# Sums over partitions by an all-ones product, square roots on ScalarE, and two running-sum products stacked into one

## The chip, the cores and the metric

One core of one Trainium2 chip runs the kernel. The metric is the device time of one execution in microseconds (us), the median of three runs.

## The reference

Two transformer blocks in a row, on 256 tokens of width 1024, in fp32. Three places matter here.

```python
# first block, state-space mixer: per head, running sums of dt*A over the tokens give the decay;
# the output is gated and normed in 8 groups of 256 channels, then multiplied by w_out
decay[i, j] = exp(cumsum[i] - cumsum[j])            # for j <= i
y = y * silu(z)
y = y * rsqrt(mean(y ** 2 over the group's 256 channels) + 1e-5) * norm_w
# second block, gated delta rule: 4 heads of 128 channels
q = l2_normalize(q) * 128 ** -0.5                   # q / sqrt(sum(q ** 2) + 1e-6)
k = l2_normalize(k)
```

Around them stand large matrix products (in-projection, two MLPs, attention, a mixture of 32 experts) whose weights come from memory once.

## The kernel before, in words

Everything is written out by hand: each engine has its own program (`block.sync`, `.scalar`, `.tensor`, `.vector`, `.gpsimd`), and they wait for one another by semaphores. Weights come in 1 MB units through a ring of six buffers. ScalarE rounds a unit to its high part (`w_hi`, line 398), VectorE subtracts to get the low part (`w_lo`, line 1656), and TensorE forms every product from three matmuls of rounded values (high by high, low by high, high by low: lines 851 to 853). Activations lie transposed, channels on partitions and tokens on the free axis, so a sum over channels is a sum over partitions.

**The scan of the state-space mixer** runs over 16 pairs of heads, hp = 0 to 15. In each step TensorE does: on every second step `scores` (lines 1004, 1005) for the next group; `running(hp + 2)` (lines 1012, 1013), which spreads each head's running sum over all partitions by a product of a picked row with the sums, once for their high and once for their low part; half a unit of the z projection (`z_half`, up to hp = 11) or a tile of the out-projection (`out_early`); `head_y(hp)` (lines 1021, 1022). VectorE forms the decay's argument (lines 1741, 1742), ScalarE its exponential (line 480), GpSimd multiplies it by the scores (line 2420), and `head_y` waits for that. ScalarE also applies silu to z (`z_read`, line 454), which needs another activation table than the exponential.

The group norm trails behind: for group g, ScalarE squares (`y_square`, line 466, odd hp), TensorE sums the squares over partitions with one column of ones as the moving operand (`group_sums`, line 1030, even hp; the result lies with tokens on partitions), VectorE scales and adds epsilon (line 1754), GpSimd raises to the power -0.5 (line 2414), TensorE turns the result and spreads it over partitions by a product with the identity (`group_scale`, line 1038, next odd hp), VectorE applies it (`y_norm`, line 1761), ScalarE and VectorE split the result (`y_high` line 471, `y_low` line 1767). `group_sums(g)` waits for `yn_done`, the end of `y_norm(g - 1)`, because both share bank 6. The last two groups are done between tiles of the out-projection.

**The delta rule** does the same for q and k: squares into `rn` (line 685; the trace shows the tile as l_rstd), 16 one-column products (line 1353), VectorE adds epsilon (line 2085), GpSimd takes the root (line 2482), and after a tile of the gate projection 16 products with the identity spread it (line 1372); VectorE applies it (line 2102). Between the two stand small running sums (line 1359) and their spread (`gb_mm`, line 1363). `gate_tile(0, 1)` stands between line 1363 and line 1372, `gate_tile(1, 0)` and `gate_tile(1, 1)` behind line 1372, and then the products of line 1385, which wait for `l2_done`.

The running sums' source `da` is written by VectorE in the softplus of unit 12 (line 1709), between two convolution units.

Of the kernel before, what the change touches and what calls it, by code (L numbers as in the profile page):

```python
# [5 lines left out]
F32 = mybir.dt.float32  # L6
# [5 lines left out]
P = 128  # L12
T = 256
# [140 lines left out]

DT_AFTER = 9
# [25 lines left out]
def build(nc, x, weights, small, consts, levels, onehot, cols, rows, ln_rows, rms_rows, b_mod, rel_bias, out):  # L181
    with ExitStack() as ctx:
# [57 lines left out]
        csT_hi = mem("sums_hi", 128, [32, T], F32R)  # L240
        csT_lo = mem("sums_lo", 129, [32, T], F32R)
        pick = mem("pick", 202, [32, 32], F32R)
# [146 lines left out]
        def _(act):  # L389
# [41 lines left out]
            A(pick[:, :], const[0:32, 0:32], ACT.Copy).then_inc(S["small_hi_done"], 1)  # L431
# [27 lines left out]
            A(csT_hi[:, :], PS[0:32, 6, 0:T], ACT.Copy).then_inc(S["csT_done"], 1)  # L459
# [21 lines left out]

            decay(0)
# [14 lines left out]
            y_square(GROUPS - 1)  # L497
            split(at("out") + 2 + AHEAD)
            y_high(6)
            y_high(7)  # L500
# [222 lines left out]
            ya_high(3)  # L723
            act.wait_ge(S["small_read"], 4 + 1)
# [121 lines left out]
        def _(pe):  # L846
# [129 lines left out]
            mm(PS[0:32, 6, 0:T], da[:, 0, :], triu_ones, start=True, stop=False)  # L976
            mm(PS[0:32, 6, P:T], da[:, 1, :], triu, start=False, stop=True).then_inc(S["small_mm"], 1)
# [29 lines left out]
            def running(hp):  # L1007

                wait(pe, S["d_read"], hp - 1)
                for c in range(2):  # L1010
                    o, one = PS[:, 2 + hp % 2, c * T:(c + 1) * T], pick[:, 2 * hp + c:2 * hp + c + 1].to_broadcast([32, P])
                    mm(o, one, csT_hi[:, :], start=True, stop=False)
                    last = mm(o, one, csT_lo[:, :], start=False, stop=True)
# [11 lines left out]
            def group_sums(g):  # L1025
                pe.wait_ge(S["sq_done"], g + 1)
                wait(pe, S["yn_done"], 2 * g)
                for t in range(TT):
                    for c in range(2):
                        last = mm(PS[:, 6, t:t + 1], ysq[:, c, t * P:(t + 1) * P], ones[:, 0:1],  # L1030
                                  start=c == 0, stop=c == 1)
                last.then_inc(S["ms_done"], 1)

            def group_scale(g):

                pe.wait_ge(S["y_rstd"], g + 1)
# [1588 lines left out]
```

## Time and profile before

| | us |
|---|---|
| median of 3 runs | 1352.01 (1351.21 to 1352.43) |
| profiled execution, its own time | 1355.23 |
| its span | 1353.4 |
| TensorE busy | 1313.4 (97%) |
| VectorE busy | 991.2 (73%) |
| ScalarE busy | 721.1 (53%) |
| GpSimd busy | 130.6 (10%) |
| mean granted TensorE clock | 0.987 of full speed |

The span is the time from the first to the last instruction of the profiled execution; the execution's own time has a little around it, and the runs without a profile are slightly shorter. A matmul in fp32 has two records in the trace, one of the rounded type one record. Records overlap, since matmuls are pipelined: the cost of one is the distance from its start to the next one's start, not its duration.

### The profile page before, as it was taken

The page shows a single profiled execution, that of the slowest core. Times are in us where ns is not written, and L with a number is a line of the kernel's source. Part 1 is how long each engine was busy: PE and PEld are TensorE (multiplying, and loading weights), DVE is VectorE, ACT ScalarE, POOL GpSimd, SP SyncE. Part 2 cuts the span into 40 slices and gives each one's busy share as a digit, 9 for nine tenths or more (in the row PEclk, how much of TensorE's full clock was granted, in tenths as well). Part 3 has the DMA queues.
Part 4 walks back from the last instruction along what each step waited for, and adds up shares of the span by engine and source line. Part 5 has one row for each costly group of instructions (what it writes and reads, how often), then busy time and mean ns, then how long its engine had stood idle before and what let it go on. Part 6 is the DMA issues. An engine that isn't in the chain of part 4 may idle for free.

```text
span 1353.4 us, 19001 instructions
## 1 busy us (share of the span) xinstructions
PE 1313.4 (97%) x8019; PEld 1151.5 (85%) x8019; DVE 991.2 (73%) x1135; ACT 721.1 (53%) x768; POOL 130.6 (10%) x118
## 2 busy tenths in 40 slices
PE   7999999999999999999999999999999999999996
PEld 7999888799998798799999798799888888888884
DVE  6978656767878735867865855747566889889896
ACT  6665764254444456544444364727324667776773
POOL 0001544200000100000000100016100000000000
PEclk9999999999999999999999998989998999999998
DMA  8543224487877543357775363421345689898992
GB/s 316 185 172 138 94 94 151 164 305 282 309 284 281 204 157 106 123 190 277 281 252 188 144 226 125 140 67 59 124 156 198 231 337 372 334 349 339 350 363 95
DMA packets 41625, 289.77 MB, mean 214 GB/s; under 512 B 4637, under 2 KB 5045, under 8 KB 7488
## 3 DMA queue, kind: packets, MB, share of 16 engines
q1 hardware_dynamic: 35712, 252.76, 50.7%
q0 software_dynamic: 5824, 35.74, 7.0%
q8 instruction: 66, 1.08, 0.3%
q14 instruction: 23, 0.19, 0.0%
HBM read 286.38 MB, written 2.11 MB: 213 GB/s over the span
## 4 chain that ended last, share of the span: by engine, by line
PE 84%; DVE 10%; ACT 3%; issue 2%; POOL 1%; DMA 0%; DVEq 0%; ACTq 0%; SPq 0%; POOLq 0%
PE banks L851 24%; PE banks L853 23%; PE banks L852 23%; DVE w_lo L1656 3%; PE banks L1419 2%; PE banks L1522 1%; ACT w_hi L398 1%; DVE conv L1702 1%; DVE qkvT L2034 1%; PE banks L1198 1%; POOL tiny L2440 1%; PE banks L1030 1%; PE banks L910 1%; DVE pre_norm L1814 1%; PE banks L1554 1%
## 5 line engine op out<-in xcount | busy, mean ns | idle before, releaser
L1656 DVE TENSOR_TENSOR w_lo<-raw,w_hi 128x2048 fp32r<-128x2048 f32 x237 | 542.2, 2295 | 110.7 <-ACT w_hi L398 109.3
L398 ACT ACTIVATE w_hi<-raw 128x2048 fp32r<-128x2048 f32 x237 | 449.9, 1909 | 17.4 <-DMA raw<-weights 17.4
L851 PE MATMUL banks<-hT_hi,w_hi 128*128 128x256 f32 x1120 | 322.6, 288 | 3.0 <-DVE w_lo L1687 3.0
L853 PE MATMUL banks<-hT_hi,w_lo 128*128 128x256 f32 x1120 | 319.7, 285 | 0.0
L852 PE MATMUL banks<-hT_lo,w_hi 128*128 128x256 f32 x1120 | 319.7, 285 | 0.0
L851 PEld LDWEIGHTS banks<-hT_hi,w_hi 128*128 128x128 f32 x1120 | 217.7, 194 | 8.3 <-issue 5.4
L852 PEld LDWEIGHTS banks<-hT_lo,w_hi 128*128 128x128 f32 x1120 | 217.8, 194 | 1.1
L853 PEld LDWEIGHTS banks<-hT_hi,w_lo 128*128 128x128 f32 x1120 | 217.7, 194 | 0.0
L851 PE MATMUL banks<-w_hi,act_hi 128*128 128x512 f32 x256 | 100.1, 391 | 0.4 <-DVE act_lo L1870 0.4
L852 PE MATMUL banks<-w_lo,act_hi 128*128 128x512 f32 x256 | 99.9, 390 | 0.0
L853 PE MATMUL banks<-w_hi,act_lo 128*128 128x512 f32 x256 | 99.6, 389 | 0.0
L851 PE MATMUL banks<-w_hi,group_T_hi 128*128 128x512 f32 x248 | 99.3, 400 | 0.0
L853 PE MATMUL banks<-w_hi,group_T_lo 128*128 128x512 f32 x248 | 97.0, 391 | 0.0
L852 PE MATMUL banks<-w_lo,group_T_hi 128*128 128x512 f32 x248 | 96.8, 390 | 0.0
L851 PE MATMUL banks<-w_hi,hT_hi 128*128 128x512 f32 (+1 forms) x240 | 90.9, 379 | 4.5 <-DVE hT_lo L1662 4.2
L853 PE MATMUL banks<-w_hi,hT_lo 128*128 128x512 f32 (+1 forms) x240 | 88.1, 367 | 0.0
L852 PE MATMUL banks<-w_lo,hT_hi 128*128 128x512 f32 (+1 forms) x240 | 88.0, 367 | 0.0
L513 ACT ACTIVATE relu<-banks 128x512 f32<-128x512 f32 x32 | 19.1, 598 | 106.2 <-PE banks L853 106.2
L1899 DVE SCALAR_TENSOR_TENSOR mod<-mod_raw,col,mod 128x512 f32<-128x512 f32 x96 | 72.1, 751 | 2.6
L2440 POOL TENSOR_TENSOR tiny<-tiny 128x1 f32<-128x1 f32 x14 | 15.5, 1107 | 587.7 <-DVE tiny L2392 315.4
L527 ACT ACTIVATE act_hi<-relu_sq 128x512 fp32r<-128x512 f32 x28 | 17.7, 633 | 87.4 <-PE banks L853 87.4
L851 PEld LDWEIGHTS banks<-w_hi,hT_hi 128*128 128x128 f32 x240 | 46.1, 192 | 14.2 <-DVE hT_lo L1662 7.0
(427 smaller groups left out, 2121.0 us busy)
## 6 DMA issues: line engine op xcount, KB each, us to landing
raw<-weights SPq DMA_DIRECT2D x238, 1024.0 KB, 4.8
mod_raw<-weights POOLq DMA_DIRECT2D x24, 1024.0 KB, 5.2
ln_gain_bias<-ln_rows POOLq DMA_DIRECT2D x4, 1024.0 KB, 8.2
h<-x SPq DMA_DIRECT2D x2, 512.0 KB, 4.3
h<-x POOLq DMA_DIRECT2D x1, 1024.0 KB, 5.5
rms_gain<-rms_rows POOLq DMA_DIRECT2D x2, 512.0 KB, 5.9
h_rows<-h POOLq DMA_DIRECT2D x1, 1024.0 KB, 4.5
bias_rows<-bias_table POOLq DMA_DIRECT2D x1, 1024.0 KB, 10.0
```

What stands on the lines that cost most here:

```text
L398: A(hi[u % RING][:, :], raw[u % RING][:, :], ACT.Copy).then_inc(S["w_hi_done"], 1)
L513: A(rbuf[e % 2][:, :], PS[:, e if e < 2 else (e + 2) % 4, :], ACT.Relu).then_inc(S["relu_done"], 1)
L527: A(aTh[e % 2][:, :, :], sbuf[e % 2][:, :].rearrange("p (c t) -> p c t", c=2), ACT.Copy).then_inc(S["act_hi"], 1)
L851: mm(out, a[0], b[0], start=start, stop=False)
L852: mm(out, a[0], b[1], start=False, stop=False)
L853: return mm(out, a[1], b[0], start=False, stop=stop)
L910: last = pe.transpose(tr_bank(0, banks + t + 2 * half)[:, c, :], source[:, t, d:d + P], ident)
L1030: last = mm(PS[:, 6, t:t + 1], ysq[:, c, t * P:(t + 1) * P], ones[:, 0:1], start=c == 0, stop=c == 1)
L1419: last = mm(tr_bank(0, b)[:, n, :], lhsT(4 * t + n), rhs(4 * t + n), start=True, stop=True)
L1656: tt(lo[u % RING][:, :], raw[u % RING][:, :], hi[u % RING][:, :].bitcast(F32), ALU.subtract).then_inc(S["w_lo_done"], 1)
L1899: last = stt(a, mraw[n % 2][:, s, :], cc["c"][:, c:c + 1], a, ALU.mult, ALU.add)
L2440: pool.tensor_tensor(rstd[:, t:t + 1], veps[:, t:t + 1], mhalf[:, 0:1], ALU.pow).then_inc(S["ln_rstd"], 1)
```

## The change

1. **Running sums stacked.** `da` is copied twice side by side (`da_twice`), so that one product puts the sums on 64 partitions instead of 32. ScalarE rounds all 64 rows at once, VectorE subtracts in the lower 32, and `pick` has 64 rows. `running` then needs one product per head instead of two.
2. **Group norm by all-ones products.** `group_sums` multiplies an all-ones square by the squares: two accumulating fp32 matmuls of 256 columns leave the sum on every partition at once. ScalarE takes the root from it: Ln with scale 1/256 and epsilon as bias, then Exp with scale -0.5. `mean_square` on VectorE, the power on GpSimd and `group_scale` on TensorE go. The wait of `group_sums` is now for the Ln of the group before. The activation table with Ln and Exp is asked for right behind each silu.
3. **Delta rule likewise.** Four all-ones matmuls of 512 columns take the place of 16 one-column products and 16 products with the identity. ScalarE takes four Ln and four Exp. The small running sums move ahead of them, and `gb_mm` between the third and the fourth.

```diff
             A(small_hi[:, :], small_raw[:, :], ACT.Copy).then_inc(S["small_hi_done"], 1)
-            A(pick[:, :], const[0:32, 0:32], ACT.Copy).then_inc(S["small_hi_done"], 1)
+            A(pick[0:32, :], const[0:32, 0:32], ACT.Copy)
+            A(pick[32:64, :], const[32:64, 32:64], ACT.Copy).then_inc(S["small_hi_done"], 1)
...
+            def y_root(g):
+                act.wait_ge(S["ms_done"], g + 1)
+                r = xbcT[:, 2 * g + 1, :]
+                A(r, PS[:, 6, 0:T], ACT.Ln, scale=1.0 / 256, bias=yrs[:, 0:1]).then_inc(S["ms_read"], 1)
+                act.wait_ge(S["ms_read"], g + 1)
+                A(r, r, ACT.Exp, scale=-0.5).then_inc(S["y_rstd"], 1)
...
             for hp in range(PAIRS):
                 if hp < PAIRS - 1:
                     decay(hp + 1)
-                if hp == 0:
-                    z_read(1)
-                if hp % 2 == 1 and hp < 12:
-                    z_read(2 + hp // 2)
+                if hp % 2 == 1 and hp >= 5:
+                    y_root((hp - 5) // 2)
+                if hp == 0 or (hp % 2 == 1 and hp < 12):
+                    z_read(2 + hp // 2 if hp else 1)
+                    act.preload_act_table_set("natural_log_exp_and_others")
...
+            act.preload_act_table_set("natural_log_exp_and_others")
+            act.wait_ge(S["l2_eps"], 1)
+            for i, n in enumerate(L2_ORDER):
+                act.wait_ge(S["l2_bc"], i + 1)
+                last = A(rn[:, 2 * n:2 * n + 2, :], PS[:, n, :].rearrange("p (c t) -> p c t", c=2), ACT.Ln,
+                         bias=l2r[:, 0:1])
+            step(last)
+            for n in L2_ORDER:
+                A(rn[:, 2 * n:2 * n + 2, :], rn[:, 2 * n:2 * n + 2, :], ACT.Exp, scale=-0.5).then_inc(S["l2_rstd"], 1)
             act.wait_ge(S["small_read"], 4 + 1)
             A(ecum, ncum, ACT.Exp, scale=-1.0).then_inc(S["small_act"], 1)
...
-                    mm(o, one, csT_hi[:, :], start=True, stop=False)
-                    last = mm(o, one, csT_lo[:, :], start=False, stop=True)
+                    last = mm(o, one, csT[:, :], start=True, stop=True)
...
             def group_sums(g):
                 pe.wait_ge(S["sq_done"], g + 1)
-                wait(pe, S["yn_done"], 2 * g)
-                for t in range(TT):
-                    for c in range(2):
-                        last = mm(PS[:, 6, t:t + 1], ysq[:, c, t * P:(t + 1) * P], ones[:, 0:1],
-                                  start=c == 0, stop=c == 1)
+                wait(pe, S["ms_read"], g)
+                for c in range(2):
+                    last = mm(PS[:, 6, 0:T], ones, ysq[:, c, :], start=c == 0, stop=c == 1)
                 last.then_inc(S["ms_done"], 1)
-
-            def group_scale(g):
...
+            def l2_sums(n):
+                pe.wait_ge(S["l2_sq"], n + 1)
+                mm(PS[:, n, :], ones, rn[:, 2 * n:2 * n + 2, :].rearrange("p k t -> p (k t)"), start=True, stop=True
+                   ).then_inc(S["l2_bc"], 1)
+
+            for n in L2_ORDER[0:3]:
+                l2_sums(n)
             pe.wait_ge(S["att_oT_lo"], SB_PAIRS + 4)
...
+            pe.wait_ge(S["small_read"], 4 + 1)
+            l2_sums(L2_ORDER[3])
             gate_tile(0, 1)
-            pe.wait_ge(S["l2_rstd"], 1)
-            pe.wait_ge(S["small_read"], 4 + 1)
...
+                    step(stt(da_all.rearrange("p (t n) -> p t n", t=TT), dt_all.rearrange("p (t n) -> p t n", t=TT),
+                             -1.0, rr["a_log"].rearrange("p (o n) -> p o n", o=1).to_broadcast([P, TT, 32]), ALU.mult,
+                             ALU.mult))
+                    for c in range(2):
+                        last = dve.tensor_copy(da_twice.rearrange("p (t o n) -> p t o n", t=TT, o=2)[:, :, c, :],
+                                               da_all.rearrange("p (t n) -> p t n", t=TT))
+                    last.then_inc(S["da_done"], 1)
```

TensorE in the scan, at the end of an even step with a group sum (before; lines 1030 sums the squares, 1004 and 1005 are `scores`, 1012 and 1013 `running`):

```order
L1030 MATMUL banks<-const,y_sq 128x1 [waits sq_done]
L1030 MATMUL banks<-const,y_sq 128x1 x3
L1004 MATMUL banks<-xbcT 128x256 [waits cb_read]
L1005 MATMUL banks<-xbcT 128x128
L1012 MATMUL banks<-sums_hi,pick 128x256 [waits d_read]
L1013 MATMUL banks<-sums_lo,pick 128x256
L1012 MATMUL banks<-sums_hi,pick 128x256
L1013 MATMUL banks<-sums_lo,pick 128x256
```

The same place after the change (other line numbers, same order):

```order
L1047 MATMUL banks<-decay_92,X 64x128
L1054 MATMUL banks<-y_sq,const 128x256 x2
L1030 MATMUL banks<-xbcT 128x256
L1031 MATMUL banks<-xbcT 128x128
L1038 MATMUL banks<-sums_parts,pick 128x256 x2
```

Four one-column products became two of 256 columns, and four products of `running` became two.

ScalarE in the scan after the change, from the exponential of one step to the next pair's (475 and 477 are the root, 458 the silu of z, 401 the rounding of a weight unit, 503 the asked-for table, 470 the squares, 482 `y_high`):

```order
L491 ACTIVATE decay_93<-decay_93 128x768 [waits d_read]
L475 ACTIVATE xbcT<-banks,tiny_147 128x256 [waits ms_done]
L477 ACTIVATE xbcT<-xbcT 128x256 [waits ms_read]
L458 ACT_TABLE_LOAD
L458 ACTIVATE zT<-banks 128x512 [waits unit_done]
L401 ACTIVATE w_hi_62<-raw_50 128x2048 [waits raw_ready1]
L503 ACT_TABLE_LOAD
L470 ACTIVATE y_sq<-zT 128x512 [waits ms_done,yg_done]
L491 ACTIVATE decay_91<-decay_91 128x768 [waits d_read]
L482 ACTIVATE yT_hi<-zT 128x256 [waits yn_done] x2
```

The two instructions of the root stand ahead of the silu's table load, and the second table load moved from behind the squares to ahead of them; their number is the same.

TensorE in the delta rule after the change (1337 and 1338 end the attention, 1363 is the small running sum, 1368 the all-ones product, 1376 `gb_mm`, 876 the gate tile):

```order
L1337 MATMUL banks<-probT_144,va 64x256 [waits att_oT_lo,att_read]
L1338 MATMUL banks<-probT_144,va 64x128
L1363 MATMUL banks<-tiny,const 128x4 [waits da_done]
L1363 MATMUL banks<-tiny,const 128x4
L1368 MATMUL banks<-l_rstd,const 128x512 [waits l2_sq] x3
L1376 MATMUL banks<-const,tiny 128x128 [waits att_oT_lo]
L1376 MATMUL banks<-const,tiny 128x128 x7
L1368 MATMUL banks<-l_rstd,const 128x512 [waits l2_sq,small_read]
L876 MATMUL banks<-w_hi_61,hT_hi 128x512 [waits w_lo_done,conv_done]
```

No product stands any more between the first and the second gate tile.

## Rows read from the trace of the kernel before

**Rows 1.** The page, part 4: the chain that ended last, by engine.
```profile
PE 84%; DVE 10%; ACT 3%; issue 2%; POOL 1%; DMA 0%; DVEq 0%; ACTq 0%; SPq 0%; POOLq 0%
```

**Rows 2.** Waits of PE, 110 to 330 us: total, times, longest.
```profile
PE banks L1030 <- DVE zT L1761: 1.9, 4, 0.6
...
PE banks L1004 <- DVE X L1728: 0.3, 1, 0.3
```

**Rows 3.** Timeline of PE in the scan: start, us, instructions.
```profile
153.82 1.05 PE L1030 MATMUL banks<-const,y_sq 128*128 128x1 f32 x8
154.73 0.68 PE L1004 MATMUL banks<-xbcT 128*128 128x256 f32 x2
155.25 0.38 PE L1005 MATMUL banks<-xbcT 128*128 128x128 f32 x2
155.56 0.38 PE L1012 MATMUL banks<-sums_hi,pick 32*128 32x256 f32 x1
155.78 0.28 PE L1013 MATMUL banks<-sums_lo,pick 32*128 32x256 f32 x1
155.90 0.28 PE L1012 MATMUL banks<-sums_hi,pick 32*128 32x256 f32 x1
...
160.10 0.71 PE L1038 MATMUL banks<-const,tiny 128*128 128x128 f32 x4
160.75 0.38 PE L1012 MATMUL banks<-sums_hi,pick 32*128 32x256 f32 x1
...
165.27 1.05 PE L1030 MATMUL banks<-const,y_sq 128*128 128x1 f32 x8
```

**Rows 4.** The same view at the scan's end, among tiles of the out-projection.
```profile
217.96 0.60 PE L1038 MATMUL banks<-const,tiny 128*128 128x128 f32 x4
218.32 0.48 PE L851 MATMUL banks<-w_hi,yT_hi 128*128 128x512 f32 x1
```

**Rows 5.** Windows, 191.4 to 196 us: busy of each engine, granted PE clock, DMA.
```profile
191.40:196.00 4.60, 4.60 (x27) 4.47 (x26) 1.39 (x4) 1.95 (x2) 2.45 (x2) 0.63 0.00 0
```

**Rows 6.** Timeline of DVE where the running sums' source is written.
```profile
100.19 0.23 DVE L1709 SCALAR_TENSOR_TENSOR da<-dt,row 128x64 f32<-128x64 f32 x1
100.34 2.28 DVE L1656 TENSOR_TENSOR w_lo<-raw,w_hi 128x2048 fp32r<-128x2048 f32 x1
```

**Rows 7.** Timeline of ACT in the scan: squares, then parts of a later pair.
```profile
161.70 0.62 ACT L466 ACTIVATE y_sq<-zT 128x512 f32<-128x512 f32 x1
...
180.22 1.28 ACT L454 ACT_TABLE_LOAD   x1
182.70 0.60 ACT L454 ACTIVATE zT<-banks 128x512 f32<-128x512 f32 x1 [1.20 <-PE banks L853]
...
188.52 0.81 ACT L471 ACTIVATE yT_hi<-zT 128x256 fp32r<-128x256 f32 x2 [0.74 <-DVE zT L1761]
```

**Rows 8.** Timeline of PE in the delta rule.
```profile
879.22 5.15 PE L1353 MATMUL banks<-const,l_rstd 128*128 128x1 f32 x32
...
885.09 3.46 PE L1363 MATMUL banks<-const,tiny 128*128 128x128 f32 x16
888.30 0.47 PE L851 MATMUL banks<-w_hi,hT_hi 128*128 128x512 f32 x1
...
891.15 3.73 PE L1372 MATMUL banks<-const,tiny 128*128 128x128 f32 x32
894.64 0.48 PE L851 MATMUL banks<-w_hi,hT_hi 128*128 128x512 f32 x1
```

**Rows 9.** Windows, 884.2 to 888.3 us, columns as in the fifth group.
```profile
884.20:888.30 4.10, 4.10 (x21) 4.10 (x22) 1.39 (x6) 0.21 (x1) 2.93 (x1) 0.52 0.00 0
```

**Rows 10.** Timeline of PE: four fp32 products of 512 columns with ones.
```profile
758.84 3.60 PE L1095 MATMUL banks<-mod,const 128*128 128x512 f32 x8
```

**Rows 11.** Timeline of DVE in the delta rule.
```profile
881.50 0.42 DVE L2051 TENSOR_TENSOR yaT_lo<-banks,yaT_hi 128x256 fp32r<-128x256 f32 x1
...
892.35 1.48 DVE L2102 SCALAR_TENSOR_TENSOR qkvT<-qkvT,banks 128x512 f32<-128x512 f32 x2 [2.55 <-PE banks L1372]
```

More of the change, by code:

```diff
@@ L152 @@
 X_BANKS = (4, 0, 2, 3)
+L2_ORDER = (1, 2, 3, 0)
 DT_AFTER = 9
@@ L497, in _ @@
             y_square(GROUPS - 1)
+            y_root(6)
             split(at("out") + 2 + AHEAD)
             y_high(6)
+            y_root(7)
             y_high(7)
@@ L1076, in _ @@
                     group_sums((hp - 4) // 2)
-                if hp % 2 == 1 and hp >= 5:
-                    group_scale((hp - 5) // 2)
             out_tile(1, 0)
@@ L1347, in _ @@
             s_values(H_A - 1)
-            for n in range(8):
-                pe.wait_ge(S["l2_sq"], n // 2 + 1)
-                for t in range(TT):
-                    last = mm(PS[:, 0, 2 * n + t:2 * n + t + 1], rn[:, n, t * P:(t + 1) * P], ones[:, 0:1],
-                              start=True, stop=True)
-            last.then_inc(S["small_mm"], 1)
-            pe.wait_ge(S["da_done"], 2)
+            pe.wait_ge(S["da_done"], 2)
+            for t in range(TT):
+                last = mm(PS[:, 0, 4 * t:4 * t + 4], triu, gdec[:, 4 * t:4 * t + 4], start=True, stop=True)
+            last.then_inc(S["small_mm"], 1)
+            def l2_sums(n):
[4 more added lines that the diff above has]
+                l2_sums(n)
             pe.wait_ge(S["att_oT_lo"], SB_PAIRS + 4)
-            for t in range(TT):
-                last = mm(PS[:, 1, 4 * t:4 * t + 4], triu, gdec[:, 4 * t:4 * t + 4], start=True, stop=True)
-            last.then_inc(S["small_mm"], 1)
             for t in range(TT):
@@ L1365, in _ @@
                 last.then_inc(S["gb_mm"], 1)
+            pe.wait_ge(S["small_read"], 4 + 1)
+            l2_sums(L2_ORDER[3])
             gate_tile(0, 1)
-            pe.wait_ge(S["l2_rstd"], 1)
-            pe.wait_ge(S["small_read"], 4 + 1)
-            for n in range(8):
-                b = (0, 1, 2, 3)[n // 2]
-                for t in range(TT):
-                    last = mm(PS[:, b, (n % 2) * T + t * P:(n % 2) * T + (t + 1) * P],
-                              l2r[:, 2 * n + t:2 * n + t + 1].to_broadcast([P, P]), ident, start=True, stop=True)
-                if n % 2 == 1:
-                    last.then_inc(S["l2_bc"], 1)
             gate_tile(1, 0)
@@ L1782, in _ @@
                     split(at("out") + hp // 2 - 6 + AHEAD)
-                if hp % 2 == 0 and hp >= 4:
-                    mean_square((hp - 4) // 2)
                 if hp % 2 == 1 and hp >= 7:
@@ L2098, in _ @@
             dve.wait_ge(S["silu_done"], 16 + 4)
-            for n in range(4):
-                dve.wait_ge(S["l2_bc"], n + 1)
+            for i, n in enumerate(L2_ORDER):
+                dve.wait_ge(S["l2_rstd"], i + 1)
                 a = qkvT[:, 2 * n:2 * n + 2, :]
-                stt(a, a, 128.0 ** -0.5 if n < 2 else 1.0, PS[:, n, :].rearrange("p (c t) -> p c t", c=2), ALU.mult,
+                stt(a, a, 128.0 ** -0.5 if n < 2 else 1.0, rn[:, 2 * n:2 * n + 2, :], ALU.mult,
                     ALU.mult).then_inc(S["l2_done"], 1)
@@ L2424, in _ @@
                     gated(hp - 1)
-                if hp % 2 == 1 and hp >= 5:
-                    y_rstd((hp - 5) // 2)
             gated(PAIRS - 1)
-            for g in range(6, GROUPS):
-                y_rstd(g)
+            pool.wait_ge(S["ms_done"], GROUPS)
             pool.dma_start(h[:, :, :], x.rearrange("(t p) d -> p t d", p=P)).then_inc(S["x_again"], 16)
```

57 lines of the change are left out of this document (19 added, 38 removed).

## Prediction

> **What bounds the kernel now.** I read the chain of waits first. It lies 84% on TensorE [rows 1], so a microsecond taken off TensorE's stream shortens the run, as long as nobody else is late in its place. Next I read TensorE's waits in the stage of the scan: 1.9 us on the wait that the change replaces, and one of 0.3 us for VectorE ahead of the scan [rows 2]. The timeline then gives the price of each kind of product, as the distance between two starts [rows 3, 4, 8, 10]. The windows show the granted clock, which halves in places [rows 5, 9]. Last I looked at what ScalarE and VectorE have spare, because ScalarE gets new work [rows 6, 7, 11].
>
> **The change, part by part.** The sums are made against the profiled execution (span 1353.4 us, own time 1355.23 us) and the difference is put on the median of the runs, 1352.0 us; a difference carries over, a total does not.
>
> *Running sums stacked.* Within `running` a product starts 0.12 us after the one before (155.78 to 155.90) [rows 3]. Two of four go in each of 16 steps: 32 x 0.118 = 3.8 us less. The remaining ones have 64 rows of contraction instead of 32. The 128-row products of the projections start at the same 0.12 us distance, so I take no extra. A doubled price would give the 3.8 us back; 0 and 3.8 are the ends, and 3.8 is the near one.
>
> *Copies of da.* VectorE's next instruction started 0.15 us after the one that writes `da` [rows 6]. Now it waits for that one's end (0.23 us) and issues two copies; I take 0.4 us in all, between 0.2 (copies hidden) and 0.7 (two full durations behind the wait). VectorE has almost no gap from there to the scan, and TensorE waits for it ahead of `scores` [rows 2], so this is on the path: 0.4 us more. The second half of `pick` (about 0.2 us of ScalarE near 21 us) is costed at nothing: TensorE does not read `pick` until the scan, and VectorE idles for TensorE and ScalarE before 95 us. Without that cover it would cost its 0.2 us.
>
> *Group sums.* Before: 153.82 to 154.73, 0.91 us [rows 3]. After: two fp32 products of 256 columns. The 16 fp32 products of 128 columns in the delta rule took 891.15 to 894.64, 0.218 us each [rows 8], so 256 columns are 0.44 us; the one of `scores` took 0.52 us with the change of operands at its start [rows 3]. I take 0.98 us, with ends at 0.88 and 1.04. Eight of them: 0.5 us more.
>
> *Group scale.* It goes. Four times it took 0.65 us (160.10 to 160.75) [rows 3], once 0.54, and three times at the end only 0.36 [rows 4], since the projection's long matmuls hide part of it: 4.2 us less.
>
> *The wait.* `group_sums` waited 1.9 us in four places for `y_norm` [rows 2]. Now it waits for the Ln of the group before, which ended a whole pair of steps earlier. What is late next is its other wait, the squares. They start 1.28 us later than before, because the table load now stands ahead of them. They ended at 162.3 us [rows 7], 2.9 us before the group sum started (165.27) [rows 3]; 1.28 of that goes to the load and about 0.9 to TensorE's own gain in that stretch, which leaves about 0.7 us. So the 1.9 us go.
>
> *ScalarE.* Each root adds an activation of 256 columns from PSUM and one from SBUF, 0.41 us each by the nearest ones (half of a pair [rows 7]); with the wait between them some 0.85 us. ScalarE waited 1.20 us for z behind its table load [rows 7], and TensorE comes 0.24 us earlier there. So the roots nearly fill the gap. As a loop: from one silu to the end of `y_high` is 188.52 + 0.81 - 182.70 = 6.6 us, set by VectorE's split and norm; then the copy of the scores and the exponential, 1.3 us; the root 0.85; the table load 1.28 [rows 7]; with hand-overs about 10.3 us. TensorE's loop was 11.45 us (from one group sum to the next, 153.82 to 165.27 [rows 3]) and becomes 11.45 - 0.47 - 0.65 + 0.07 = 10.4 us, 10.3 or less where the wait was. It is a tie. z has two banks, so ScalarE can be late by a fraction of a microsecond over four pairs with no wait on TensorE. I cost it at nothing.
>
> *The clock in the scan.* At 191.4 to 196 us the granted clock is 0.63 of full speed [rows 5], a mix of the 1.2 and 2.4 GHz levels; it costs up to 4.6 x 0.37 = 1.7 us, and I take 1.5. Ahead of it stood the wait of 0.4 us, one-column products, fp32 scores and `running`. The same sequence two and four steps earlier brought no fall, so it was a near thing, and now the wait and the one-column products are gone from it. I take the fall away: 1.5 us less.
>
> *Delta rule.* Before, from the start of the one-column products to the second gate tile: 879.22 to 894.64, 15.4 us [rows 8], of which some 6 us at the 1.2 GHz level, to which the clock fell in the middle of the one-column products [rows 9]. After, all at 2.4 GHz: small sums 0.5; three all-ones products at 4 x 0.218 = 0.87 us (four such in the trace took 3.60 us together, 0.90 each [rows 10]), 2.6; `gb_mm`, 8 x 0.218 = 1.75; the fourth 0.87; the gate tile 2.85 (888.30 to 891.15) [rows 8]. Sum 8.6 us, 6.8 us less. The wait ahead of `gb_mm` is for a VectorE instruction that ended at 881.92 [rows 11]; TensorE comes there at 879.22 + 0.5 + 2.6 = 882.3, so nothing. Behind it ScalarE does four Ln to about 885.7, four Exp to about 888, the small Exp, and VectorE then applies four times 0.74 us [rows 11], done near 891.5. TensorE needs that after two more gate tiles, at 879.2 + 8.6 + 5.6 = 893.4. Two microseconds cover it. Everything behind is moved forward whole.
>
> GpSimd loses nine short instructions that nobody waits for now; the load of x that stands behind them can go out sooner, in the shade of the out-projection.
>
> **Sum:** -3.8 + 0.4 + 0.5 - 4.2 - 1.9 - 1.5 - 6.8 = -17.3 us, so 1352.0 - 17.3 = **1334.7 us**.
>
> **The rivals.**
>
> *A: the fall of the clock in the scan stays* or turns up in another place of the scan. Against it: the denser stream. For it: it came without a visible cause. Time: 1334.7 + 1.5 = 1336.2.
>
> *B: ScalarE becomes the bound of the scan.* If root and hand-overs take 1.5 us instead of 0.85, its loop is 11.0 us against TensorE's 10.3, and after four pairs the squares are late: 4 x 0.7 = 2.8, 1337.5. For it: the tie above. Against: the two banks of z and 0.7 us of room. The trace's table load takes 1.28 us [rows 7]. The Trainium skill ("ScalarE: Activation LUTs", the section on table sets) budgets about 2.7 us for one; by that figure ScalarE's loop would be 2.8 us longer, 13.1 us, and the scan slower than before instead of faster. The trace disagrees with it, and the measured load decides.
>
> *C: the clock in the delta rule falls as before*, near 881.7 us, and is back only six microseconds later. Then 2.5 us of the 8.6 run at full speed, the next 6.3 us do 3.15 us of work and the last 2.9 run full: 11.7 us, a gain of 3.7 instead of 6.8. Time: 1337.8. Against it: it fell during one-column products, which are gone; ahead of the new products stand only 0.8 us of the attention's short ones and 0.5 us of small sums.
>
> *D: slower.* If Ln and Exp did not share a table set, each root would bring two more loads: 8 x 2 x 1.28 = 20.5 us on ScalarE's loop, which is already even with TensorE's. 1334.7 + 20.5 = 1355.2. It decides from 17.3 / 8 = 2.2 us per root. Against it: in the order of the built program no load stands between exponential, Ln and Exp, and their number is unchanged.
>
> *E: part of the change does nothing.* If contraction over 64 rows costs double, 3.8 us come back: 1338.5. The projections' 128 rows at the same price speak against it.
>
> *F: more than forecast*, because the other falls of the clock (near 830 and 1030 us) get shorter as well: 1331 to 1333. Nothing in those stages changes.
>
> **How the numbers follow.** Forecast 0.57 (within 1.5 us, the spread of the small terms), A 0.14, B 0.11, C 0.09, E 0.02, F 0.04, D 0.02, and 0.01 for a change within 0.2%, which is about what a measurement of this kernel can tell from none (2.7 us). The range reaches from 1331.0, inside F, to 1339.0, past B, C and E with a microsecond of spread, and leaves out two of them together. Faster 0.97, same 0.01, slower 0.02.
>
> **What would show it.** In the new profile: two starts per `running`, 0.12 us apart; group sums of 0.95 to 1.0 us; no wait of TensorE at them; a granted clock of 1.0 from 180 to 230 us and around the delta rule; second gate tile some 8.6 us behind the end of the attention; ScalarE's wait for z near zero. A wait of TensorE for the squares would show B, a clock below 1 beside the all-ones products C. I am wrong if the gain of the scan, from the start of the first `scores` to the last group sum, is under 7 us, or that of the delta rule under 5.

## The result and the profile after

The change takes 1338.34 us in the median of 4 runs (1334.0 to 1340.29), against 1351.61 us (1350.9 to 1352.43, 4 runs) for the kernel before. The ratio is 0.9895, with a 95% interval of 0.9875 to 0.9914. So it is faster by 13.3 us, inside the range and 3.6 us slower than the forecast, outside the 1.5 us that the prediction had allowed around it. The profiled execution took 1340.29 us, its span 1338.5 us, 14.9 us less than the span before.

Line numbers of the kernel after: 876 to 878 are the three matmuls of a rounded product, 1030 and 1031 `scores`, 1038 `running`, 1046 and 1047 `head_y`, 1054 the group sum, 475 and 477 the root, 470 the squares, 458 silu, 482 `y_high`, 491 the exponential, 1766 `y_norm`, 2416 GpSimd's product of decay and scores, 1363, 1368 and 1376 the small sums, the all-ones products and `gb_mm` of the delta rule.

Part 4 of the page after, the chain that ended last, by engine:

```profile
PE 81%; DVE 10%; issue 3%; ACT 2%; POOL 2%; DMA 1%; DVEq 0%; SPq 0%; POOLq 0%; ACTq 0%
```

TensorE still holds the chain, with 81% instead of 84% [rows 1]; GpSimd has 2% instead of 1%. The timeline of TensorE in the scan after, with start and duration in us, answers to [rows 3]:

```profile
151.34 1.13 PE L1054 MATMUL banks<-y_sq,const 128*128 128x256 f32 x4
152.31 0.59 PE L1030 MATMUL banks<-xbcT 128*128 128x256 f32 x2
```

From start to start the group sum costs 0.97 us, where 0.98 was forecast. `running` has its products 0.12 us apart where they follow one another, and the group scale is gone. But the waits of TensorE from 110 to 240 us (in total, times, longest, in us) answer to [rows 2] like this:

```profile
PE banks L1046 <- POOL decay L2416: 2.8, 3, 1.2
PE banks L1054 <- ACT y_sq L470: 1.6, 2, 1.0
PE banks L1009 <- DVE conv L1708: 0.6, 1, 0.6
PE banks L1030 <- DVE X L1738: 0.4, 1, 0.4
```

The wait for `y_norm` (1.9 us) is gone, and two new ones of 4.4 us together stand in its place: `head_y` waits for GpSimd's product, and the group sum for the squares. The timeline of TensorE in the delta rule after answers to [rows 8]:

```profile
872.91 0.61 PE L1363 MATMUL banks<-tiny,const 128*128 128x4 f32 x4
873.38 2.82 PE L1368 MATMUL banks<-l_rstd,const 128*128 128x512 f32 x6
876.04 1.95 PE L1376 MATMUL banks<-const,tiny 128*128 128x128 f32 x16
877.82 1.02 PE L1368 MATMUL banks<-l_rstd,const 128*128 128x512 f32 x2
...
881.45 0.39 PE L876 MATMUL banks<-w_hi,hT_hi 128*128 128x512 f32 x1
```

From the attention's end to the second gate tile it is 8.5 us (8.6 forecast) instead of 15.4. So the 14.9 us between the two spans are made up like this:

| stretch, by the start of the instruction that ends it | before | after | difference |
|---|---|---|---|
| start to first `scores` | 124.46 | 123.58 | -0.9 |
| to the last group sum (228.04, 220.52) | 103.58 | 96.94 | -6.6 |
| to the delta rule (879.22, 872.91) | 651.18 | 652.39 | +1.2 |
| to the second gate tile (894.64, 881.45) | 15.42 | 8.54 | -6.9 |
| to the end of the span | 458.76 | 457.05 | -1.7 |

The scan (the second row) should have given 3.8 + 4.2 + 1.9 + 1.5 - 0.5 = 10.9 us. It gave 6.6. The missing 4.3 us are matched by the 4.4 us of new waits.

**Where the new waits come from.** The next three views are timelines of the same microseconds of the kernel after, around one `y_norm`: VectorE, GpSimd, ScalarE. The bracket at a row's end is the idle time before it and who ended it.

```profile
171.62 0.75 DVE L1772 TENSOR_TENSOR yT_lo<-zT,yT_hi 128x256 fp32r<-128x256 f32 x2
172.29 2.42 DVE L1766 SCALAR_TENSOR_TENSOR zT<-zT,col,xbcT 128x256 f32<-128x256 f32 x2
174.64 0.47 DVE L1751 SCALAR_TENSOR_TENSOR decay<-banks,tiny,const 128x256 f32<-128x256 f32 x1
```

```profile
172.14 1.91 POOL L2416 TENSOR_TENSOR decay<-decay,cb 128x768 f32<-128x768 f32 x1 [3.02 <-ACT decay L491]
...
184.18 1.91 POOL L2416 TENSOR_TENSOR decay<-decay,cb 128x768 f32<-128x768 f32 x1 [4.46 <-ACT decay L491]
```

```profile
174.36 0.81 ACT L482 ACTIVATE yT_hi<-zT 128x256 fp32r<-128x256 f32 x2 [2.30 <-DVE zT L1766]
...
176.06 0.85 ACT L491 ACTIVATE decay<-decay 128x768 f32<-128x768 f32 x1 [0.51 <-DVE decay L1752]
```

The pair of `y_norm` took 2.42 us. It began 0.15 us after GpSimd's product and ended only 0.66 us after that product's end at 174.05. Elsewhere in the same kernel the same pair takes 0.87 us (161.30 and 208.18), where it starts ahead of GpSimd's product or has none beside it. Three of the eight pairs are held like this (at 172.29, 184.34 and 196.39), 1.55 us each, 4.7 us in all. In the list of line 1766 (duration in ns: least, median, most) the spread is plain; the same list of the kernel before is the second:

```profile
L1766 DVE SCALAR_TENSOR_TENSOR zT<-zT,col,xbcT x16: 471/477/2037, 161.3 to 224.4; 128x256 f32<-128x256 f32 x16
```

```profile
L1761 DVE SCALAR_TENSOR_TENSOR zT<-zT,col,banks x16: 469/475/481, 164.0 to 232.7; 128x256 f32<-128x256 f32 x16
```

The names tell the difference. Before, `y_norm` read z from SBUF, the large on-chip memory, and the scale from PSUM (`banks`), the small one that TensorE writes its products to. After, the root is written to SBUF (`xbcT`), and `y_norm` reads both tensors there. No other operand changed. In the kernel before the same neighbours met too, GpSimd's product first and `y_norm` 0.16 us behind it, and the pair kept its 0.87 us:

```profile
187.85 1.92 POOL L2420 TENSOR_TENSOR decay<-decay,cb 128x768 f32<-128x768 f32 x1 [3.03 <-ACT decay L480]
```

```profile
188.01 0.87 DVE L1761 SCALAR_TENSOR_TENSOR zT<-zT,col,banks 128x256 f32<-128x256 f32 x2
```

The Trainium skill ("SBUF — State Buffer", the section "Who interferes with whom") says that a VectorE instruction with two SBUF inputs contends with a GpSimd instruction that reads SBUF; the section "SBUF: two separate sides" adds that the one that starts first holds the shared ports for its whole instruction while the other stands still. The trace agrees: 0.87 us alone, 2.42 us behind the start of a product of 1.91 us.

The kernel before shows the same hold, on other instructions with two tensors in SBUF. Its timelines of GpSimd, then of VectorE (the split of a weight unit, line 1656, which reads only SBUF):

```profile
128.46 5.68 POOL L2420 TENSOR_TENSOR decay<-decay,cb 128x768 f32<-128x768 f32 x2 [127.63 <-ACT decay L480]
...
207.31 2.84 POOL L2409 TENSOR_TENSOR zT<-y_skip,zT 128x256 f32<-128x256 f32 x1
```

```profile
128.66 3.79 DVE L1656 TENSOR_TENSOR w_lo<-raw,w_hi 128x2048 fp32r<-128x2048 f32 x1
...
207.26 2.29 DVE L1656 TENSOR_TENSOR w_lo<-raw,w_hi 128x2048 fp32r<-128x2048 f32 x1 [0.63 <-ACT w_hi L398]
```

The split started 0.20 us behind GpSimd's product and took 3.79 us, where alone it takes 2.28 [rows 6]. At 207 us it was the other way: VectorE started first, its split kept its 2.29 us, and GpSimd's sum of 256 columns took 2.84 us, where 0.73 is its usual time (213.67). These rows stood in the trace that the prediction was made from, which read neither them nor the rule.

The delta rule moved the same operand, and there it cost nothing. VectorE's last step on q and k read the scale from PSUM before [rows 11] and reads it from SBUF (`l_rstd`) now:

```profile
882.14 2.50 DVE L2101 SCALAR_TENSOR_TENSOR qkvT<-qkvT,l_rstd 128x512 f32<-128x512 f32 x4
```

That is 0.62 us for each, where the prediction took 0.74. GpSimd runs nothing from 863 to 888 us, so nobody is there to hold it.

### The profile page after: what moved, and what is told of

Same layout as the page of the kernel before. It is cut to its first block, busy times and chain, and to the rows that moved or that the text cites. A ratio compares the mean times of both kernels' runs of the same rounds, so it can differ in the third digit from the quotient of the medians.

```text
span 1338.5 us, 18708 instructions
## 1 busy us (share of the span) xinstructions
PE 1297.3 (97%) x7867; PEld 1132.2 (85%) x7867; DVE 993.2 (74%) x1128; ACT 731.5 (55%) x793; POOL 118.8 (9%) x111
## 4 chain that ended last, share of the span: by engine, by line
PE 81%; DVE 10%; issue 3%; ACT 2%; POOL 2%; DMA 1%; DVEq 0%; SPq 0%; POOLq 0%; ACTq 0%
PE banks L876 24%; PE banks L878 23%; PE banks L877 23%; DVE w_lo L1662 3%; PE banks L1425 2%; PE banks L1528 1%; DVE conv L1708 1%; DMA raw<-weights 1%; POOL decay L2416 1%; DVE qkvT L2035 1%; ACT w_hi L401 1%; PE banks L1209 1%; POOL tiny L2433 1%; PE banks L935 1%; DVE pre_norm L1815 1%
## 6 DMA issues: line engine op xcount, KB each, us to landing
bias_rows<-bias_table POOLq DMA_DIRECT2D x1, 1024.0 KB, 11.2
```

## The experiments

**Theory.** The new waits come from `y_norm` being held by GpSimd through its new operand. It reaches TensorE over ScalarE, where `y_high`, the exponential and the squares stand in one line behind it. **Rivals:** the root itself has made ScalarE too slow; or the squares are late only because the table load now stands ahead of them; or the gain was never there, and one of the three parts is worth less than the sum says. Intervals of small effects overlap in places, and where they do it is said.

### The change once more

> The changed kernel once more, as the base for the others on the same chip. The trace of the change shows VectorE's pair of norm products (line 1766) at 2.4 us instead of 0.87 in three pairs of the scan, each time beside GpSimd's product of decay and scores, ScalarE waiting 2.3 us for it, and TensorE waiting 1.6 us for the squares and 2.8 us for GpSimd. Every theory expects the same again here: a median between 1334 and 1340 us.

1338.76 us (1337.28 to 1339.9) against 1352.59 us before (11 runs), ratio 0.9891 (0.9869 to 0.9913). Its profile has the same two waits, 2.8 and 1.6 us. The result repeats, and the waits belong to the kernel.

### `y_norm` earlier on VectorE

```diff
                 skip(hp)
+                if hp % 2 == 1 and hp >= 5:
+                    y_norm((hp - 5) // 2)
                 if hp == 0:
                     split(at("in", 17) + AHEAD)
...
                 if hp % 2 == 1 and hp >= 7:
                     y_low((hp - 7) // 2)
-                if hp % 2 == 1 and hp >= 5:
-                    y_norm((hp - 5) // 2)
```

> y_norm stands ahead of the weight split on VectorE instead of behind y_low, so it no longer runs when GpSimd's product starts. Theory 1 (VectorE reads two SBUF tensors there and is held up by GpSimd's work on SBUF, and that delay goes through y_high into ScalarE's loop): the pair takes 0.9 us, ScalarE's wait for it goes, TensorE's waits for squares and decay go from 4.4 to under 1 us, and the time falls by 3.5 to 4.5 us against the change. Theory 2 (ScalarE simply has too much work with the roots and the table loads, the slow norm only fills a gap): VectorE's pair gets short but TensorE still waits over 3 us, and the time falls by under 1 us.

1333.77 us (1331.43 to 1336.46), ratio 0.9862 (0.9838 to 0.9886). That is 5.0 us less than the change beside it by the medians. The intervals of the two ratios overlap a little (0.9869 to 0.9913 for the change), but no single run of the one lies among those of the other, and the gain came twice: once more beside other kernels it was 1334.65 us (1333.15 to 1336.45) against 1352.45, ratio 0.9867 (0.9847 to 0.9887). The expectation of the second run:

> y_norm ahead of the split once more, as base for the two below on the same chip: about 5 us faster than the change, some 1333 to 1335 us.

TensorE's waits from 110 to 240 us in the first of them:

```profile
PE banks L1009 <- DVE conv L1708: 0.6, 1, 0.6
PE banks L1030 <- DVE X L1738: 0.4, 1, 0.4
PE banks L1046 <- POOL decay L2416: 0.3, 1, 0.3
```

and VectorE's timeline, two `y_norm` of neighbouring pairs of steps:

```profile
178.41 1.37 DVE L1766 SCALAR_TENSOR_TENSOR zT<-zT,col,xbcT 128x256 f32<-128x256 f32 x2
...
188.74 1.35 DVE L1766 SCALAR_TENSOR_TENSOR zT<-zT,col,xbcT 128x256 f32<-128x256 f32 x2
```

Of the 4.4 us of waits 4.1 are gone. The pair now falls beside a shorter GpSimd instruction and takes 1.37 us, still more than the 0.9 that was expected (one pair, at 196.27, took 2.18). From the first `scores` (123.45) to the last group sum (215.84) it is 92.4 us, 4.5 less than in the change and 11.2 less than in the kernel before, where the prediction's terms for the scan make 10.9. The second profile has the same 92.4. More telling is the distance between the two: 10.33 us, against 12.05 in the change (172.29 to 184.34). ScalarE does the same work as in the change, root and table loads included, and keeps up with 10.33. So the root has not made ScalarE too slow; that rival falls. By itself, though, this run doesn't say whether the hold or the place in VectorE's order was to blame, because the split of the weight unit, 2.3 us, also no longer stands ahead of `y_norm`.

### The root in PSUM, `y_norm` where it was

```diff
                 act.wait_ge(S["ms_read"], g + 1)
-                A(r, r, ACT.Exp, scale=-0.5).then_inc(S["y_rstd"], 1)
+                A(PS[:, 6, T:2 * T], r, ACT.Exp, scale=-0.5).then_inc(S["y_rstd"], 1)
...
-                wait(pe, S["ms_read"], g)
+                wait(pe, S["yn_done"], 2 * g)
```

and `y_norm` reads `PS[:, 6, T:2 * T]`. The bank is shared with the group sum, so the wait for `y_norm` comes back.

> The Exp of the root writes into the second half of PSUM bank 6 and y_norm reads it there, as it did before the change, in the old place behind y_low; group_sums waits for the norm of the group before again, since both share the bank. Theory 1: the norm's pair takes 0.9 us although it still runs beside GpSimd, since only one of its tensors lies in SBUF; TensorE's waits for squares and decay fall under 1 us, up to 2 us of the old wait for the norm come back, and the time falls by 2 to 4 us against the change. Theory 2: no change beyond 1 us. If the pair stays at 2.4 us here, the second SBUF tensor isn't the reason.

1340.67 us (1337.97 to 1342.83, 6 runs), ratio 0.9908 (0.9887 to 0.9929): no gain over the change. But the views show both halves of it. VectorE's and GpSimd's timelines at the same place as above:

```profile
184.39 0.87 DVE L1766 SCALAR_TENSOR_TENSOR zT<-zT,col,banks 128x256 f32<-128x256 f32 x2
```

```profile
184.24 1.91 POOL L2416 TENSOR_TENSOR decay<-decay,cb 128x768 f32<-128x768 f32 x1 [3.03 <-ACT decay L491]
```

GpSimd's product starts 0.15 us ahead of `y_norm`, as in the change, and `y_norm` takes 0.87 us instead of 2.42. Same instruction, same neighbour, one operand in another memory: that shows the hold. The longest of all 16 took 481 ns. What was won is lost to the wait that had to come back, in TensorE's waits:

```profile
PE banks L1054 <- DVE zT L1766: 7.6, 7, 1.5
```

The expectation was right on the instruction and on the waits for squares and decay, which are gone. It missed the returning wait (7.6 us, not up to 2) and with it the time, which did not fall.

### Squares ahead of the table load

```diff
                     z_read(2 + hp // 2 if hp else 1)
-                    act.preload_act_table_set("natural_log_exp_and_others")
...
                 if hp % 2 == 1 and hp >= 3:
                     y_square((hp - 3) // 2)
+                if hp == 0 or (hp % 2 == 1 and hp < 12):
+                    act.preload_act_table_set("natural_log_exp_and_others")
```

> The squares stand ahead of the table load on ScalarE again. Both theories: TensorE's 1.6 us wait for the squares goes. Theory 1: ScalarE's loop is as long as before, so the delay only moves to the decay's product: TensorE waits about as long in all, and the time falls by under 1 us. A rival, that the table load ahead of the squares is the whole trouble, expects 3 to 4 us.

1338.6 us (1334.69 to 1340.1, 6 runs), ratio 0.9889 (0.9867 to 0.9911), no different from the change. TensorE's waits:

```profile
PE banks L1047 <- POOL decay L2417: 3.2, 2, 2.3
```

(`head_y` and the product of decay, one line further down in this kernel). The wait for the squares, 1.6 us, is gone, and the one for GpSimd grew from 2.8 to 3.2, with one of 2.3 us among them: 3.2 us in all instead of 4.4. Two neighbouring `y_norm` lie as far apart as in the change, 12.04 us (172.29 to 184.33). Being late in a loop shows where the loop is read first; taking away one place of it mostly moves the wait. The load's place is not the cause.

### Each part alone

The kernel before was profiled again in the same batch. Each of the next three kernels has one of the three parts of the change and is otherwise the kernel before: `running` with its copies and `pick` alone, the group norm alone, the delta rule alone.

> The kernel before once more, for a second profile. If the fall of the clock near 191 us in the scan is a property of that sequence, it is here again; if it hangs on chance, it is elsewhere or missing.

> Only the stacked running sums, all else as before. The sum of the prediction gives -3.8 us for 32 products and +0.4 us for the copies of da, so 3.4 us faster than before. The rival that contraction over 64 rows costs double expects 0.4 us slower.

> Only the group norm by the all-ones product with the root on ScalarE, all else as before. By the sum of the prediction +0.5 -4.2 -1.9 = 5.6 us faster (7.1 with the clock's fall in the scan gone). By theory 1 (the norm's second SBUF tensor is held up by GpSimd) VectorE's pair takes 2.4 us here too and TensorE waits 2 to 4 us for squares and decay, so 2 to 4 us faster; TensorE has more to do per pair here than in the full change, so the waits are shorter than its 4.4 us.

> Only the delta rule's part, all else as before. The sum of the prediction and the trace of the change (15.4 us became 8.5 us from the end of the attention to the second gate tile) both say 6.9 us faster than before. If the rest of the stage gives some back, less.

| kernel | median us (runs) | ratio, 95% interval | against before |
|---|---|---|---|
| before, in this batch | 1351.52 (18) | | |
| running sums stacked | 1349.04 (11) | 0.9983 (0.9971 to 0.9995) | -2.5 |
| group norm | 1345.26 (5) | 0.9956 (0.9942 to 0.9969) | -6.3 |
| delta rule | 1347.29 (8) | 0.997 (0.996 to 0.9981) | -4.2 |

The three make 13.0 us, the whole change 13.3. So the parts add up, within intervals of 1.4 to 1.8 us on either side of each. The edit of each is its part of the diff ahead of the prediction; of the first, this much is the core:

```diff
-                    mm(o, one, csT_hi[:, :], start=True, stop=False)
-                    last = mm(o, one, csT_lo[:, :], start=False, stop=True)
+                    last = mm(o, one, csT[:, :], start=True, stop=True)
```

of the second:

```diff
-                wait(pe, S["yn_done"], 2 * g)
-                for t in range(TT):
-                    for c in range(2):
-                        last = mm(PS[:, 6, t:t + 1], ysq[:, c, t * P:(t + 1) * P], ones[:, 0:1],
-                                  start=c == 0, stop=c == 1)
+                wait(pe, S["ms_read"], g)
+                for c in range(2):
+                    last = mm(PS[:, 6, 0:T], ones, ysq[:, c, :], start=c == 0, stop=c == 1)
```

and of the third:

```diff
+            for n in L2_ORDER[0:3]:
+                l2_sums(n)
...
+            l2_sums(L2_ORDER[3])
             gate_tile(0, 1)
```

*Running sums.* TensorE's waits, first of the kernel before in this batch, then of this one:

```profile
PE banks L1030 <- DVE zT L1761: 1.8, 4, 0.6
```

```profile
PE banks L1031 <- DVE zT L1766: 2.7, 4, 0.8
```

The wait for `y_norm`, still there in this kernel, grew by 0.9 us. A faster TensorE came sooner to somebody who had not become faster. That would be most of the difference between 3.4 us (3.8 less the copies' 0.4) and 2.5; the interval, 0.7 to 3.9 us, is too wide to tell the two apart.

*Group norm.* VectorE's timeline, `y_norm` only:

```profile
164.11 0.87 DVE L1754 SCALAR_TENSOR_TENSOR zT<-zT,col,xbcT 128x256 f32<-128x256 f32 x2
175.57 2.43 DVE L1754 SCALAR_TENSOR_TENSOR zT<-zT,col,xbcT 128x256 f32<-128x256 f32 x2
187.63 2.44 DVE L1754 SCALAR_TENSOR_TENSOR zT<-zT,col,xbcT 128x256 f32<-128x256 f32 x2
```

The hold is there with the group norm alone, three times with 2.4 us (another at 199.68), and with it the loop of 12.05 us. Its TensorE waits 3.0 us for GpSimd and the squares, where the change waits 4.4. That TensorE waits the more in the change fits its shorter stream there.

But the gain, 6.3 us with an interval of 4.2 to 7.8, is more than the 2 to 4 us expected, so that expectation was missed. The scan isn't where the surplus lies: from the first `scores` to the last group sum the profile has 99.29 us instead of 103.58, 4.3 less, and 5.6 + 1.5 for the clock less 3.0 of waits makes 4.1. Part of it lies behind the delta rule. From the second gate tile to the end the five profiles with the old group norm took 457.1 to 458.8 us, the nine with the new one 455.4 to 457.1. Why, no run shows.

*Delta rule.* 4.2 us, by the interval between 2.6 and 5.4 us, where 6.8 were summed. Why, the next part says.

### The kernel before, three profiles of it

> A third profile of the kernel before. The first has the fall of the clock near 191 us and 15.4 us from the end of the attention to the second gate tile, the second no such fall and 13.8 us there. If chance decides how long the clock stays down, the third differs from both; at full clock that stretch would be 12.0 us.

The windows of the second and the third profile of the kernel before (busy time and instructions of PE, PEld, DVE, ACT and POOL, then the granted clock, the DMA share and GB/s):

```profile
192.00:196.00 4.00, 4.00 (x34) 3.03 (x33) 0.83 (x2) 2.79 (x4) 1.36 (x2) 1.00 0.42 129
...
880.00:884.00 4.00, 4.00 (x32) 4.00 (x32) 1.43 (x6) 0.57 (x2) 2.01 (x1) 0.83 0.02 4
884.00:888.00 4.00, 4.00 (x17) 3.45 (x17) 1.90 (x8) 2.25 (x3) 0.92 (x1) 0.74 0.00 0
```

```profile
192.00:196.00 4.00, 4.00 (x24) 3.86 (x24) 0.88 (x3) 1.34 (x2) 1.83 (x2) 0.61 0.00 0
```

The profile of before that the prediction read had 0.63 at this place of the scan [rows 5] and 0.52 in the delta rule [rows 9]. The second has 1.00 and, for two windows, 0.83 and 0.74; the third has 0.61 in the scan. So the fall in the scan came in two profiles of three, and the one in the delta rule comes in all three but not with the same length. TensorE's timeline in the second and in the third, from the one-column products to the second gate tile:

```profile
877.96 3.73 PE L1353 MATMUL banks<-const,l_rstd 128*128 128x1 f32 x32
...
891.73 0.48 PE L851 MATMUL banks<-w_hi,hT_hi 128*128 128x512 f32 x1
```

```profile
876.99 3.73 PE L1353 MATMUL banks<-const,l_rstd 128*128 128x1 f32 x32
...
890.79 0.48 PE L851 MATMUL banks<-w_hi,hT_hi 128*128 128x512 f32 x1
```

13.8 us in both, against 15.4 in the first [rows 8], where the one-column products alone took 5.15 us instead of 3.73. So the third did not differ from both, as the expectation would have it if chance decided. From 880 to 890 us the granted clock was 0.66 in the first profile and 0.83 in the other two, which costs 3.4 us against 1.7. The first profile held the longest fall of the three. The gain over a usual execution is 13.8 - 8.5 = 5.3 us, which lies in the interval of the delta rule alone.

### The better versions

Two more were made of what had been learned: the early `y_norm` with the squares ahead of the table load, and the early `y_norm` with the root in PSUM. Their edits are those shown above, put together.

> y_norm ahead of the split and the squares ahead of the table load. With the norm's delay out of ScalarE's loop, TensorE waits only 0.3 us in the scan, so theory 1 expects no difference to norm_early2 (within 0.5 us). A rival, that the order of squares and table load costs on its own, expects 1 us or more.

> y_norm ahead of the split and its second operand in PSUM. Theory 1: the pair takes 0.87 us in all eight places instead of 1.4 to 2.2 us in four or five, and group_sums' wait for the norm costs nothing, since the norm is done long before. TensorE already waits only 0.3 us, so within 0.5 us of norm_early2.

| kernel | median us (range) | ratio, 95% interval |
|---|---|---|
| before, in this batch | 1352.45 (1349.15 to 1355.25) | |
| early `y_norm` | 1334.65 (1333.15 to 1336.45) | 0.9867 (0.9847 to 0.9887) |
| with squares first | 1332.48 (1330.94 to 1333.98) | 0.985 (0.983 to 0.9869) |
| with root in PSUM | 1336.5 (1330.83 to 1337.05) | 0.9872 (0.9851 to 0.9893) |

The one with the squares first has the lowest median of all, 20.0 us below before. Its interval overlaps with that of the early `y_norm` alone, and from the first `scores` to the last group sum both take the same 92.4 us. So nothing shows that the squares' place adds something in the scan, and the 2.2 us between the medians stay without a cause. With the root in PSUM the pair takes 0.87 us in all eight places, as expected, but the wait of `group_sums` is not free: TensorE waits again for `y_norm`, and the scan takes 93.9 us.

```profile
PE banks L1054 <- DVE zT L1766: 1.4, 1, 1.4
```

## Why the prediction was right, and where it was not

**Running sums, -3.8 us: right.** Two starts per `running`, 0.12 us apart; rows of 64 cost what rows of 32 did. Rival E is refuted. Alone, the part gave 2.5 (0.7 to 3.9); 0.4 goes to the copies and some 0.9 to the wait that still stood there.

**Copies of da, +0.4 us: right.** From TensorE's products of `da` to the first `scores` it was 124.46 - 109.82 = 14.64 us and became 123.58 - 108.50 = 15.08, 0.44 more. It comes as longer waits for VectorE: those for the convolution and for X, 1.0 us after, 0.6 before.

**Group sums and group scale: right, but for a small slip.** 0.97 us for 0.98, and the scale is gone. The term of 0.5 us took all eight at that price. The last two, among tiles of the out-projection, went from 0.81 to 0.67 us, so all eight together cost 0.1 us more than before, not 0.5. **The old wait: right**, it does not show in the waits after.

**ScalarE costed at nothing: this step failed.** The prediction took ScalarE's loop as 10.3 us, with 6.6 of them from silu to the end of `y_high`, read in the profile before. In that profile `y_norm` had an operand in PSUM. With it in SBUF the pair takes 2.4 us instead of 0.87, and the 1.5 us more go into that very stretch. 10.3 + 1.5 = 11.8, and measured were 12.05 us per pair of steps. The other way round, 12.05 less the 1.55 of the hold leaves 10.5 us. That is an estimate from these rows, since no run has this order without the hold and without another wait. Of the 0.2 us above the forecast, 0.1 is the root: from its start to the next instruction's it took 0.93 us (164.61 to 165.54), not 0.85. The version with `y_norm` early doesn't measure this loop, since its `y_norm` no longer stands behind the split; its 10.33 us show that ScalarE's own work fits into TensorE's loop. So the count of ScalarE's work was nearly right, and it lacked a price for the new neighbour. The price shows as 4.4 us of waits in the profile, where three holds of 1.55 make 4.7; between the change and the early `y_norm` it is 4.5 us by the scans and 5.0 us by the medians. The last two have the new place of `y_norm` in them, since no run takes the hold alone away without bringing a wait back.

In its outcome this is rival B (ScalarE's loop longer than TensorE's, 1337.5 us, with a chance of 0.11), though not for B's reason: not root and hand-overs, but `y_norm` ahead of `y_high`. The sign that the prediction named for it, a wait of TensorE for the squares, is there, and 1338.3 us lies nearer to B's 1337.5 than to the forecast. The table loads took 1.28 us in the profile after as well, and the next activation started 1.30 us behind the start of one (177.73 to 179.03), so nothing longer stands in the loop for them.

**The clock in the scan, -1.5 us: right in its place, and given back further on in this pair of profiles.** Neither profile of the change has a fall from 180 to 230 us, as forecast. But the window of the profile after shows one 50 us later, in the out-projection's end and the norm behind it:

```profile
248.00:256.00 8.00, 6.36 (x40) 6.36 (x41) 5.71 (x10) 0.42 (x1) 1.52 (x1) 0.79 0.29 121
```

It costs up to 8 x 0.21 = 1.7 us, and the stretch between scan and delta rule was 1.2 us longer. All fourteen profiles, counted by the granted clock of their windows, show a pattern:

| profiles | fall at 192 to 196 us | fall between 244 and 260 us |
|---|---|---|
| five with the old group norm | 4 (0.60 to 0.68) | 1, in the one that has none at 192 |
| nine with the new group norm | 1 (0.57) | 7, that one among them |

The two that have neither are the early `y_norm` in its first run and the version with the squares first as well; in its second run the same early `y_norm` has one (0.71 at 244 to 248 us). The first run of the early `y_norm` has one at 750 to 760 us (0.83) instead. So where the fall leaves the scan, it mostly comes later. The table counts one place only: three of the five with the old group norm have a second fall in the scan (0.67 and 0.63 at 204 to 208 us, 0.68 at 176 to 180), and none of the nine has one there. From 120 to 270 us that makes eight falls in five profiles against eight in nine, at some 1.7 us each, so on average the new stream has about 0.7 of a fall less. This is rival A a little further on: that rival had the fall turn up in another place of the scan, at a price of 1.5 us. What sets the place wasn't tried and stays open.

**Delta rule, -6.8 us: right in its mechanism, too large in one term.** The length after was 8.5 for 8.6, and the granted clock is 1.0 there in every profile of a kernel with this part; rival C is refuted. What failed is the length before: 15.4 us was the longest of three, and 13.8 would have given 5.3. The prediction's bound of 5 us for this part was kept, barely.

**Rival D** (more table loads) is refuted by the time alone. **Rival F** finds nothing in the two profiles compared: the granted clock is 0.89 from 820 to 850 us and 0.90 from 1010 to 1060 us in both. Over many executions it stays open.

**The sum again:** -17.3, with 4.4 us given back by the waits, 1.5 by the delta rule and 1.2 by the later fall of the clock, is -10.2. Measured are -13.3, by the interval between 11.6 and 16.9. Some 3 us of the gain are thus accounted for by no step, and without them the time would have been about 1341.8 us, outside the range. That the number came out inside is luck to this extent. In the two profiles the start and the tail are 2.6 us shorter, where the change edits nothing that the sum counts but the copies. The start took 124.5, 123.1 and 124.5 us in the three profiles of the kernel before, so one pair of profiles says little of it; the shorter tail comes in the kernels with the new group norm, as said above. Its cause stays open. The prediction had said it would be wrong if the scan gained under 7 us. It gained 6.6. So by its own mark it was wrong on the scan, although its number came out in the range.

## What to carry to other kernels

When the result of an elementwise step moves from PSUM to SBUF, look up who reads it, where that reader's other operand lies, and what GpSimd does at that time; take the price from a row where two such instructions already meet: here it stood in the trace before. A step that is ready early should stand ahead of a long one in its engine's order, above all if another engine's loop goes through it. Before a slow clock in a profile is counted as a gain, take a second profile of the same kernel, and look whether the fall only moves.

## What the runs showed of the hardware

- A VectorE instruction of 256 fp32 columns with both tensors in SBUF takes 0.48 us alone and up to 2.04 us when it starts behind a GpSimd product of 768 columns (1.91 us). With one tensor in PSUM it takes at most 0.481 us at the same place.
- It goes both ways: GpSimd's sum of 256 columns took 2.84 us instead of 0.73 when it started 0.05 us behind a split of VectorE, which kept its 2.29 us.
- The same stretch of the same kernel took 15.4, 13.8 and 13.8 us in three profiles, and the granted clock from 880 to 890 us was 0.66, 0.83 and 0.83. At one place of the scan it was 0.63, 1.00 and 0.61.
